# Routing kept on the chip, a gate in a dead buffer, and a spill of x in two pieces

## What is computed

```
x = first_block(...)                      # ends with rms_norm(x, final_norm)
x = x + (g_a * y_a + g_b * y_b) @ w_out   # second block, mixers
h = rmsnorm(x, norm2_g)
g_logits = h @ w_rg + b_rg                # 4 groups
g_sel    = argmax(g_logits);  p_group = softmax(g_logits)[g_sel]
e_in_group = (h @ w_re + b_re).reshape(n_tok, 4, 8)[:, g_sel]
top_val, top_idx = top_k(e_in_group, 2)
weights  = p_group * softmax(top_val)
for e in range(32):
    he = silu(h @ w_gate_e[e]) * (h @ w_up_e[e])
    y += combine[:, e:e+1] * (he @ w_down_e[e])
```

## Time and profile before

| | before |
|---|---|
| median of three runs | 3001.38 us |
| profiled execution, its own time | 3002.19 us |
| its span | 3000.9 us |
| PE matmul busy | 2712.9 us (90%) |
| PE weight load busy | 2152.0 us (72%) |
| DVE busy | 1829.4 us (61%) |
| ACT busy | 1221.3 us (41%) |
| GpSimd busy | 281.4 us (9%) |

### The profile page before, as it was taken

The page is one execution under the profiler, slowest core; times in us unless marked ns, Lnnn a source line. Parts: engine busy times, 40 slices in busy tenths (PEclk is TensorE's granted clock), DMA queues, the critical chain, the costliest instruction groups (busy, mean ns, idle before and its releaser), DMA issues. The chain is left out here.

```text
span 3000.9 us, 42987 instructions
## 1 busy us (share of the span) xinstructions
PE 2712.9 (90%) x18210; PEld 2152.0 (72%) x18210; DVE 1829.4 (61%) x2231; ACT 1221.3 (41%) x1557; POOL 281.4 (9%) x204
## 2 busy tenths in 40 slices
PE   8889999999999799999999898868898877599996
PEld 6667878888766388788888786646777656488885
DVE  6765455445578564554545665276567544499997
ACT  4444243223433442332324332143443323488884
POOL 1001010000100020100001000022012001223221
PEclk9999999999999799999999999978999888699998
DMA  4213222222211032222322343211011053499995
GB/s 158 83 61 118 98 85 98 99 99 89 94 56 43 23 118 98 85 98 95 101 86 99 130 157 107 110 48 25 16 26 23 11 202 130 168 396 367 385 374 229
DMA packets 88430, 366.74 MB, mean 122 GB/s; under 512 B 26032, under 2 KB 30256, under 8 KB 54320
## 3 DMA queue, kind: packets, MB, share of 16 engines
q1 hardware_dynamic: 78192, 339.33, 31.8%
q0 software_dynamic: 10048, 24.66, 2.5%
HBM read 346.62 MB, written 39.35 MB: 129 GB/s over the span
## 5 line engine op out<-in xcount | busy, mean ns | idle before, releaser
L479 PE MATMUL bank<-xg_hi,w_hi 128*128 128x512 f32 x1504 | 598.7, 398 | 20.9 <-DVE xg_lo L501 11.9
L479 PE MATMUL bank<-xg_hi,w_lo 128*128 128x512 f32 x1504 | 587.9, 391 | 0.0
L479 PE MATMUL bank<-xg_lo,w_hi 128*128 128x512 f32 x1504 | 587.9, 391 | 0.0
L466 DVE TENSOR_TENSOR w_lo<-w_raw,w_hi 128x2048 fp32r<-128x2048 f32 x165 | 378.7, 2296 | 199.1 <-ACT w_hi L462 198.8
L462 ACT ACTIVATE w_hi<-w_raw 128x2048 fp32r<-128x2048 f32 x165 | 314.2, 1905 | 250.3 <-PE bank L479 204.1
L479 PEld LDWEIGHTS bank<-xg_hi,w_hi 128*128 128x128 f32 x1504 | 284.1, 189 | 85.8 <-DVE w_lo L466 14.5
L479 PEld LDWEIGHTS bank<-xg_lo,w_hi 128*128 128x128 f32 x1504 | 284.0, 189 | 64.2 <-issue 5.9
L479 PEld LDWEIGHTS bank<-xg_hi,w_lo 128*128 128x128 f32 x1504 | 283.7, 189 | 59.8
L2946 DVE TENSOR_TENSOR w_lo<-e_w_raw,w_hi 128x2048 fp32r<-128x2048 f32 x77 | 174.5, 2285 | 10.5 <-ACT w_hi L2768 10.5
L2768 ACT ACTIVATE w_hi<-e_w_raw 128x2048 fp32r<-128x2048 f32 x77 | 147.7, 1918 | 29.1 <-PE bank L479 29.1
L479 PE MATMUL bank<-f_h_hi,w_hi 128*128 128x512 f32 x384 | 151.7, 395 | 0.0
(11 more groups left out here) (466 smaller groups left out, 5216.1 us busy)
## 6 DMA issues: line engine op xcount, KB each, us to landing
w_raw<-stream SPq DMA_DIRECT2D x165, 1024.0 KB, 4.8
e_w_raw<-expert_rows SPq DMA_DIRECT2D x63, 1024.0 KB, 9.5
w_raw<-expert_rows SPq DMA_DIRECT2D x33, 1024.0 KB
y_rows<-e_y_row SPq DMA_DIRECT2D x39, 512.0 KB
p_spill<-p_stage SPq DMA_DIRECT2D x36, 256.0 KB, 2.0
mix_gate<-p_spill SPq DMA_DIRECT2D x16, 256.0 KB, 4.3
na_bias<-bias_na SPq DMA_DIRECT2D x16, 224.0 KB, 4.3
rw_rkv<-p_spill SPq DMA_DIRECT2D x12, 256.0 KB, 6.7
```

The lines of the kernel that those rows point to most:

```text
L466: V.tensor_tensor(ring(m)["lo"][m % SLOTS][:, :], ring(m)["raw"][m % RAW][:, :], ring(m)["hi"][m % SLOTS][:, :].bitcast(F32), ALU.subtract ...
L479: return T.matmul(out_ap, lhsT, rhs, start=first, stop=last, skip_group_check=True)
```

## The change

Four edits. The third weight unit is split at the start, ahead of the first norm's root and reciprocal. The gate of head 4 goes to `ab_tmp[0]` and is scaled right behind `head(4)`. The final norm scales tiles 0 to 2 of x before the second reciprocal, and x is stored in two pieces, the first of these three tiles. The routing makes its table without DRAM: a scan over the choices replaces eleven of the fourteen rank matmuls, two one-hot arrays (place of the token in its block, and its block times the token's number) are multiplied by eight fp32 matmuls, and DVE copies the result to `e_table`; ACT scales four tiles of h ahead; the exponentials go behind the copies.

```diff
 def _expert_consts():
-    c = {"before": p[:, None] < p[None, :], "one32": np.ones((P, 32)),
+    c = {"before_less_one": (p[:, None] < p[None, :]) - 1.0, "one32": np.ones((P, 32)),
...
+         "place": np.broadcast_to(np.arange(P), (P, P)), "block_id": np.broadcast_to(np.arange(BLOCKS), (P, BLOCKS)),
+         "tile_seg": np.broadcast_to(np.arange(P) % 4 != 0, (P, P))}
...
+        with ExitStack() as under:
+            e_place = sb(under, "e_at_place", [P, 8, P])
         e_h_hi, e_h_lo = sb(ph, "e_h_hi", [P, 2, KT, P], F32R), sb(ph, "e_h_lo", [P, 2, KT, P], F32R)
...
     def new_splits(n):
-            return range(2 if n == 0 else n, n + SLOTS)
+            return range(SLOTS if n == 0 else n, n + SLOTS)
...
     def sp_take(Y, n):
-        for m in ([0, 1] if n == 0 else []) + list(new_splits(n)):
+        for m in (list(range(SLOTS)) if n == 0 else []) + list(new_splits(n)):
...  act_start, after the eight squares; dve_start, between split 1 and dve_norm_rstd
+        act_split(A, 2)
+        dve_split(V, 2)
...
+    ab_gate_of = [ab_tmp[0][:, :] if h == 4 else ab_gate[:, h % 4, :] for h in range(8)]
...  (ab_gate[:, h % 4, :] becomes ab_gate_of[h] on ACT and DVE)
         def gate(h):
             V.wait_ge(*pe_ab.at("gate", h))
-            if h >= 4:
+            if h == 4:
+                V.wait_ge(*dve_ab.at("yb_lo", 2))
+            elif h > 4:
                 V.wait_ge(*dve_ab.at("y_lo", h - 4))
...
         head(4)
+        gate(4)
         gated(3)
         dve_take(V, out_b[0])
         multipliers(ab_halves[0])
         dve_take(V, out_b[1])
         add_b(0, 1)
         output(0)
-        gate(4)
         add_b(2, 3)
...
     def dve_final_norm(V):
...
-        V.wait_ge(*act_norm.at(7, "root"))
-        V.reciprocal(rstd[:, :], square[:, 1, :]).then_inc(*dve_norm.mark(7, "rstd"))
         V.wait_ge(*dve_final.at("r"))
         for j in range(KT):
+            if j == 3:
+                V.wait_ge(*act_norm.at(7, "root"))
+                V.reciprocal(rstd[:, :], square[:, 1, :]).then_inc(*dve_norm.mark(7, "rstd"))
             stt(V, x[:, j, :], x[:, j, :], vcol("final", j), root[:, :], ALU.mult, ALU.mult)...
...
     def sp_second(Y):
+        Y.wait_ge(*dve_final.at("x", 2))
+        Y.dma_start(x_spill[:, 0:3, :], x[:, 0:3, :]).then_inc(*x_spilled[0].mark("x"))
         Y.wait_ge(*dve_final.at("x", KT - 1))
-        Y.dma_start(x_spill, x[:, :, :]).then_inc(*x_spilled.mark("x"))
+        Y.dma_start(x_spill[:, 3:, :], x[:, 3:, :]).then_inc(*x_spilled[1].mark("x"))
...  (act_second and dve_second wait for x_spilled[0]; sp_mixers waits for x_spilled[1] before it loads the masks)
+    def h_tile(j):
+        return e_place[:, 4 * j:4 * j + 4, :].rearrange("p a b -> p (a b)") if j < 2 else square[:, (j + 1) % 2, :]
...
     def sp_experts(Y):
-        Y.wait_ge(*dve_e.at("table_zero"))
-        Y.dma_start(table_rows, e_table).then_inc(*table_dma.mark("cleared"))
...
-        Y.wait_ge(*scatter_dma.at(1, 3))
-        Y.dma_start(e_table, table_rows).then_inc(*table_dma.mark("table"))
...
     def pe_experts(T):
         project(T, router_unit, 2 * P, 0, ring2["xg"], range(KT), b, pe_e, ("router",), xg_ready(8))
+        for j in range(2):
+            pe_rows_of_tile(T, j)
...  (logits and col as before)
-        for j in range(KT):
+        for j in range(2, 6):
             pe_rows_of_tile(T, j)
-        b = take_bank(T, ("ranks",), dve_e, "rank")
-        T.wait_ge(*dve_e.at("both"))
+        b = take_bank(T, ("ranks",), dve_e, "rank_in_block")
+        T.wait_ge(*dve_e.at("so_far"))
-        for t in range(4):
-            o = b[:, t * 32:(t + 1) * 32]
-            for u in range(t):
-                matmul(T, o, const("ones"), r_both[:, u, :], u == 0, False)
-            matmul(T, o, econst("before"), r_both[:, t, :], t == 0, True)
-        for t in range(4):
-            mm = matmul(T, b[:, P:P + 32], const("ones"), r_both[:, t, :], t == 0, t == 3)
-        mm.then_inc(*pe_e.mark("ranks"))
+        matmul(T, b[:, 0:P], econst("before_less_one"), flat(r_both), True, False)
+        matmul(T, b[:, 0:P], const("ones"), flat(r_so_far), False, True)
+        matmul(T, b[:, P:P + 32], const("ones"), r_so_far[:, :, 3]).then_inc(*pe_e.mark("ranks"))
+        for j in range(6, KT):
+            pe_rows_of_tile(T, j)
+        b = take_bank(T, ("table",), dve_e, "table")
+        T.wait_ge(*dve_e.at("of_block"))
+        for i in range(8):
+            mm = matmul(T, b[:, 0:BLOCKS], r_at_place[:, i, :], r_of_block[:, i, :], i == 0, i == 7)
+        mm.then_inc(*pe_e.mark("table"))
         pe_turn_rows(T, 0)
...
     def act_experts(A):
-        A.wait_ge(*normed(8))
-        A.wait_ge(*dve_e.at("g_less"))
+        for j in range(4):
+            act_h_tile(A, j)          # tile 3 waits for logits, tile j >= 4 for rows j - 2
+        for j in range(KT):
+            act_rows_of_tile(A, j)    # now the four copies alone
+            if j + 4 < KT:
+                act_h_tile(A, j + 4)
+        A.wait_ge(*dve_e.at("v_less"))
         A.activation(r_g_tmp, r_g_tmp, ACT.Exp).then_inc(*act_e.mark("g_exp"))
...
     def dve_choose(V):
-        V.wait_ge(*act_e.at("g_exp"))
-        V.tensor_reduce(r_p_group, r_g_tmp, AX_X, ALU.add).then_inc(*dve_e.mark("g_sum"))
+        V.tensor_tensor(by_group, el.rearrange("p t (g e) -> p t g e", g=4), of_group, ALU.mult)...
         V.wait_ge(*dve_e.now())
-        for g in range(N_GROUPS):     # product and sum of each group, seven instructions
+        V.tensor_reduce(r_e8, by_group.rearrange("p t g e -> p t e g"), AX_X, ALU.add)...
...
-        V.wait_ge(*act_e.at("w2_exp"))     # four instructions on the weights, now in dve_weights
+        for c, one in enumerate((r_one1, r_one2)):
+            V.tensor_tensor(r_choice[c]..., one.unsqueeze(2).to_broadcast([P, 4, 4, 8]), of_group, ALU.mult)...
+        V.tensor_tensor(r_both.rearrange("p e t -> p t e"), r_choice[0], r_choice[1], ALU.add)...
+        V.tensor_tensor_scan(flat(r_so_far), econst("tile_seg"), flat(r_both), 0.0, ALU.mult, ALU.add)...
...
     def dve_place_rows(V):           # the waits between dependent instructions left out here
+        ts(V, r_beyond, rank, float(P), None, ALU.is_ge)            # rank, count: read in PSUM
+        ts(V, r_blocks, count, float(P + 1), None, ALU.is_ge)
+        for m in range(2, 4): stt(V, r_quot, rank, ...); stt(V, r_blocks, count, ...)
+        stt(V, r_rank, r_quot, -float(P), rank, ALU.mult, ALU.add)
         V.tensor_tensor_scan(r_ended, econst("one32"), r_blocks, 0.0, ALU.mult, ALU.add)
+        V.tensor_tensor(r_over[0]..., r_choices, flat(r_rank)..., ALU.mult)              # 256
+        V.tensor_reduce(r_rank_of, r_over[0].rearrange("p (i e) -> p i e", i=8), AX_X, ALU.add)
+        V.tensor_tensor(r_at_place, r_rank_of..., econst("place")..., ALU.is_equal)      # 1024
         ...  (spare_at, spare_block, if_beyond, block_at as before)
+        V.tensor_tensor(r_over[1]..., r_choices, flat(r_quot)..., ALU.mult)              # 256
+        V.tensor_reduce(r_block_of, r_over[1].rearrange("p (i e) -> p i e", i=8), AX_X, ALU.add)
+        V.tensor_tensor(r_of_block, r_block_of..., econst("block_id")..., ALU.is_equal)  # 312
+        for c in range(2): V.tensor_tensor(half, half, econst("token")..., ALU.mult)     # 156
         ...  (slot, owners, owner, w_index as before)
+        V.wait_ge(*pe_e.at("table"))
+        V.tensor_copy(e_table, held("table")[:, 0:BLOCKS]).then_inc(*dve_e.mark("table"))
...
     def pool_experts(G):
-        G.wait_ge(*table_dma.at("cleared"))
-        G.wait_ge(*dve_e.at("slot"))
-        for c in range(2):
-            for t in range(4):
-                G.indirect_dma_start(slot_table, bass.IndirectOffsetOnAxis(
-                    ap=e_slot[:, 4 * c + t:4 * c + t + 1], axis=0), e_tok[:, t:t + 1], None)...
         G.wait_ge(*h_store.at(3))
-        G.wait_ge(*table_dma.at("table"))
-        G.wait_ge(*dve_e.at("w_index", 2))
+        G.wait_ge(*dve_e.at("table"))
```

More of the change, by code:

```diff
@@ L388, in build @@
     dve_final = line("dve_final_norm")
-    x_spilled = dma_line("x_spill_store")
+    x_spilled = [dma_line(f"x_spill_store{i}") for i in range(2)]
     p_store = [dma_line(f"p_store{i}") for i in range(STAGES)]
@@ L2887, in dve_place_rows @@
     def dve_place_rows(V):
-        for c, one in enumerate((r_one1, r_one2)):
-            for g in range(N_GROUPS):
-                V.tensor_tensor(r_choice[c][:, :, 8 * g:8 * g + 8], one, per_tile(r_g_one[:, :, g:g + 1], 8),
-                                ALU.mult).then_inc(*dve_e.mark("choice", c, g))
-        V.wait_ge(*dve_e.now())
-        V.tensor_tensor(r_both, r_choice[0], r_choice[1], ALU.add).then_inc(*dve_e.mark("both"))
-        V.wait_ge(*pe_e.at("ranks"))
-        V.tensor_copy(r_count, held("ranks")[:, P:P + 32]).then_inc(*dve_e.mark("count"))
@@ L2896, in dve_place_rows @@
[L2896 to L2904 removed]
+        count = held("ranks")[:, P:P + 32]
@@ new lines, in dve_place_rows @@
```

(22 more changed lines are left out.)

144 lines of the change are left out of this document (76 added, 68 removed).

## The result

| | before | after |
|---|---|---|
| median of the runs shown with the result | 3001.47 us (4 runs) | 2949.38 us (4 runs) |
| ratio, with its 95% interval | | 0.9824, from 0.9807 to 0.9841 |
| profiled execution, and its span | 3002.19, 3000.9 | 2946.86, 2945.4 |
| the whole change once more, on another chip | 3005.12 (9 runs) | 2946.71 (5 runs), ratio 0.9809, from 0.9796 to 0.9823 |

The forecast was 2943.6 with a range from 2936 to 2954. Both medians lie in the range, 5.8 and 3.1 us above the forecast. (Beside the second, the kernel before had 3005.12, and less 57.8 that would be 2947.3.) The profiled executions differ by 55.3 us, and 57.8 was forecast for them.

The account below looks back on a forecast made before the run. PE, busy 90%, was taken as the bound, so its waits cost. Start 3.9, gate 13.4, norm 8.8 and routing 31.7 sum to 57.8 us, taking the median from 3001.4 to 2943.6, range 2936 to 2954.

Parts of the forecast that it names:

- The rival in which heads 5 to 7 give the gate's time back: First mixer: DVE's output chain can't start earlier, so heads 5 to 7 wait; whole gate gain lost, 2957 us; chance 0.09.
- The margin that I called just sufficient: First mixer, heads 5 to 7: DVE wins back 3 x 4.6 = 13.8 us, against PE 13 us ahead.
- The store's landing: Final norm: the first piece, three eighths of the bytes, lands after 4 us, between 2.4 and 6.3.
- (c): Routing, ranks: 3 matmuls with 6 weight loads take 1.4 us; DVE reads the ranks at 2542.9.
- (d): Routing, place: 21 DVE instructions to the second one-hot product take 6.7 us and end at 2549.6.
- (e): Routing, table: 8 matmuls with 16 loads take 3.6 us, a copy 0.2; done at 2553.4.
- (f): Routing, rows of h: last copy about 2547; from 2548.7, 2 MB at 391 GB/s take 5.4 us, to 2554.1.
- (g): Routing: GpSimd starts the gather 0.8 us later, at 2554.8 instead of 2586.45, 31.7 us earlier.
- the first rival: Routing: the store of h, at half pace 10.7 us, sets the gather; routing gives 26.4, total 2949 us; chance 0.12.
- Two us or more after the table: Routing, sign of a wrong forecast: the rows' store releases the gather 2 us or more after the table.
- The rule against the strided operations: Routing: each access to a new SBUF or PSUM line pays; six strided DVE operations add 1.7 us, sum 56.1.
- The rival in which it becomes bound by DMA: Expert phase: late units or rows make blocks 11.1 us instead of 9.5, 62 us over 39 blocks, 3006; chance 0.02.

Follow-up runs that it names:

- the gate's: The kernel before with only the gate of head 4 moved; 2991.78 us (5 runs), ratio 0.9955.
- the norm's: The kernel before with only the final norm's edit and the store of x in two pieces; 2997.04 us (8 runs), ratio 0.9973.
- the routing's kernels: The kernel before with every routing hunk and none of the other three parts; 2972.78 us (4 runs), ratio 0.9886.
- five of six units: The whole change with five expert weight units loaded before the store of h rows and the sixth behind; 2946.12 us (5 runs), ratio 0.9809.
- four won half a us at most: The whole change with four expert weight units loaded before the store of h rows and two behind; 2947.46 us (5 runs), ratio 0.9815.
- two lost 2.5 or more: The whole change with two expert weight units loaded before the store of h rows and four behind; 2950.79 us (5 runs), ratio 0.982.
- the kernel whose store had an empty queue ahead of it: The whole change without h scaled ahead, all transposes of h behind the logits again; 2957.21 us (4 runs), ratio 0.9848.

## Why the prediction was right, step by step

**The start and the gate.** Both held to half a us: 3.5 for 3.9, 13.9 for 13.4. The 13.9 lie just past the better end that I had given (13.6), as do the 9.15 of the norm (9). The rival in which heads 5 to 7 give the gate's time back did not occur. The margin that I called just sufficient did suffice, and the shift is constant through the three heads. What the outputs took back, 0.5 to 0.8 us, I had at nothing. The start's 3.5 are 2.5 at the split of unit 2, forecast 2.2, and 1.0 at `ab_tmp`, forecast 1.7: that wait did not go, it shrank to 0.7. I had no term for the clock behind the `w_lo` wait. The kernel before was granted 1.00 there in its profiled execution, but the gate's, the norm's and the routing's kernels, which keep that wait, were granted 0.50 for some 3 us behind it. Against those three, from the same matmul ahead of the wait, the start's edit gives 4.1. So that both terms held to half a us is in part luck: the same edits give 4.1 and 12.8 against other executions without them.

**The norm.** It gave 9.15 for 8.8. The store's landing was taken at 4 between bounds of 2.4 and 6.3; it is 3.9. This store is not paid in proportion to its bytes: three eighths of them took 0.62 of the time.

**The routing** gave 29.15 for 31.7. Counted from the last norm's last split (2524.92 in the kernel before, 2497.78 after), the steps are:

| step | forecast | measured |
|---|---|---|
| (c) ranks read | 18.0 | 18.6 |
| (d) 21 DVE operations, to the second one-hot product | 24.7 | 24.9 |
| (e) table copied | 28.5 | 28.9 |
| (f) last byte of the rows | 29.2 | 28.7, and one engine to 31.1 |
| (g) gather | 29.9 | 32.2 |
| first expert matmul | 41.3 | 43.8 |

The forecast of each row is its time there less 2524.92; the last is the gather and 11.42. The chain of choice, ranks, place and table, built from two rows of DVE durations, is off by 0.2 to 0.6 us at each of its steps, over 28.9. The step that failed in size is (f) to (g). I had the rows' last byte at 29.2 and the gather 0.7 behind it. The bulk of the bytes ended a little sooner than that, at 28.7 or before, but one of the sixteen engines worked on to about 31.1, and the gather came 1.1 behind it. It is the first rival by its place, the store of h setting the gather, but not by its reason: the engines moved 414 GB/s up to 2526 and never went at half pace before the tail. "Two us or more after the table" stood among the signs of a wrong forecast. From the table's copy at 2526.48 it is 3.5 us, so that sign did appear. Its price is 2.4 us, the gather at 32.2 where the table alone would have let it go at 29.8; released by the table, it would have met the forecast of 29.9. These 2.4 are nearly all that the routing gave less than forecast (2.5).

The Trainium skill ("DMA: Bandwidth & Descriptors", section "Why a DMA increments its semaphore by 16 and not by 1") says that a transfer's sixteen engines finish independently and that only all sixteen mean that the data is there. The trace agrees: the release comes behind the engine that ends last, with the share at 0.06 before it.

**The rule against the strided operations** (the Trainium skill, "SBUF — State Buffer", section "Door 1: The DMA port swizzle") gives no price; twice the plain one was my reading. Measured, the steps cost almost nothing. The write across experts took 0.385 us and the reduction across experts 0.376, where a plain product of 128 columns took 0.284 to 0.293: 0.09 each. The four strided reads of the ranks in PSUM took 0.287 to 0.292, the plain price. Six operations cost 0.2 us more, where that reading had 1.7. The rows, from the list of DVE's groups by shape for 2505 to 2530 us:

```profile
L2898 DVE TENSOR_TENSOR e_routing<-e_routing 128x128 f32<-128x128 f32 x1 | 0.4, 385 | 0.0
L2882 DVE TENSOR_REDUCE e_routing<-e_h_row 128x32 f32<-128x128 f32 x1 | 0.4, 376 | 0.0
L2951 DVE TENSOR_TENSOR e_routing<-e_routing 128x128 f32<-128x128 f32 x1 | 0.3, 292 | 0.0
L506 DVE TENSOR_SCALAR e_routing<-bank 128x128 f32<-128x128 f32 x1 | 0.3, 290 | 1.6 <-PE bank L481 1.6
```

**The expert phase** did what was said: it began earlier and did not change, 386.1 us from the first expert matmul to the last matmul before and 386.6 after. The rival in which it becomes bound by DMA did not occur.

**The median.** The two comparisons gave 52.8 and 57.4 us, where 57.8 was forecast and the trace shows 55.7 at the edits. What the first lacks is not explained by anything in the one trace that goes with it; its interval, 0.9807 to 0.9841, reaches from 48 to 58 us.

## What to carry to other kernels

Where two chains meet at one wait, price both to the moment at which the waiting engine moves: for a store that means its last engine and the release behind it (1.1 to 1.2 us here, some 3.5 from the end of the bulk), not the end of its bytes. A transfer that stands ahead of the critical one can be moved behind it, but only so much that it has landed before the next critical one starts: five of six units won 1.8 to 2.2 us, four won half a us at most and two lost 2.5 or more. When a view names who released a wait, look in the kernel what the instruction waits for: here it named an operation that nothing waited for, and the store only seemed to be off the path. And a stall that is taken off one engine is worth its whole length when the trace shows that the next engine in the chain has waits to win back; count those before calling it hidden.

## What the runs showed of the hardware

In the whole change one of sixteen DMA engines finished about 2.5 us behind the others when the store stood behind six loads of 1 MB. In the other execution of the same kernel the share ran down over 2 us (0.79, 0.55, 0.34 and 0.14 in the half microseconds from 2528.5), and in the kernel whose store had an empty queue ahead of it there was no such tail. The packets in the traces say why. A weight unit moves in packets of 8 KB (0.31 us each), the rows in packets of 4 KB (0.16 us), 512 of them, so 32 to an engine or 5.0 us. In the whole change nearly all engines had left the weights for the rows by 2521.5, but one packet of weights at a time ran on until 2523.80. The last packet of rows ended at 2528.79, 5.0 us later. In the other execution 14, 8, 6, 3 and no engines were still on weights at 2523.8 and each half microsecond after, and 14, 10, 6, 3 and none on rows from 2528.8 on. The trace does not name the engine of a packet, so that it is the same engines follows from the counts alone. With eleven more rank matmuls the store was issued when the six units were through (2525.64, their last packet 2525.39). Counted from the last norm's last split it was issued 3.6 us later than in the whole change, and it had landed only 1.0 later.

In that kernel PE's granted clock, 0.50 while the extra rank matmuls kept PE busy from 2518 to 2522, was back at 1.00 in the midst of the routing, and lower again while PE waited for the place, with nothing to run. In the whole change, without these matmuls, it stayed at 0.50 from 2510 to the gather. The stretches of the kernel with more matmuls (PEclk is the third column from the end):

```profile
2518.00:2522.00 4.00, 4.00 (x21) 4.00 (x21) 0.00 (x0) 1.89 (x8) 0.00 (x0) 0.50 1.01 426
2522.00:2524.00 2.00, 1.84 (x14) 1.60 (x13) 1.02 (x7) 0.56 (x3) 0.00 (x0) 0.84 0.80 336
2524.00:2526.00 2.00, 0.00 (x0) 0.00 (x0) 2.00 (x8) 1.98 (x8) 0.00 (x0) 1.00 0.15 61
2526.00:2528.00 2.00, 0.00 (x0) 0.00 (x0) 1.86 (x6) 1.22 (x3) 0.00 (x0) 0.51 0.78 315
```
